# One 512 KB weight load moved from SyncE's DMA queue to ScalarE's, in a one-core hybrid attention layer

## The reference, cut to what matters

```
h   = rmsnorm(x, norm_pre_g)
u   = h @ w_in                       # 1024 x 4096: q, k, v and gate columns of two head groups
A   = differential attention, B = block-sparse attention, both with a relative position bias
y   = concat(A * silu(gate_a), B * silu(gate_b)) @ w_out
out = x + rmsnorm(y, norm_post_g)
```

## Time and profile before

| | |
|---|---|
| median of 3 runs | 254.0 us (253.83, 254.0, 255.63) |
| the profiled execution | 254.23 us |
| its span | 252.4 us |
| PE busy | 245.6 us, 97% of the span |
| DVE, ACT, POOL busy | 177.0, 143.0, 32.7 us |
| mean granted TensorE clock | 0.997 |
| DMA moved | 42.47 MB |

### The profile page before, as it was taken

How to read it: one execution, slowest core, us unless ns; L and a number is a source line. 1 busy time by engine, 2 the same in 40 slices (tenths; PEclk the granted TensorE clock), 3 DMA queues, 4 the chain that set the end, 5 groups by cost and what they waited for, 6 DMA issues and landing times.

```text
span 252.4 us, 4450 instructions
## 1 busy us (share of the span) xinstructions
PE 245.6 (97%) x1567; PEld 123.2 (49%) x1567; DVE 177.0 (70%) x393; ACT 143.0 (57%) x336; POOL 32.7 (13%) x74
## 2 busy tenths in 40 slices
PE   8999999999999999999999999999999999999991
PEld 6454444445444554544455444454444444555570
DVE  2998585587478688868877767977787896835313
ACT  4777565375356666574677595667565665611110
POOL 1329300000000320041031033000000000111101
PEclk9999999999999999999999999999999999999998
DMA  6978979605656545544935644568849869982422
GB/s 242 366 245 173 310 251 371 218 28 135 106 160 163 180 114 130 140 163 112 203 103 136 137 161 119 136 189 184 174 103 201 209 157 170 202 203 43 125 86 83
DMA packets 59674, 42.47 MB, mean 168 GB/s; under 512 B 45808, under 2 KB 46072, under 8 KB 59652
## 3 DMA queue, kind: packets, MB, share of 16 engines
q1 hardware_dynamic: 59636, 42.18, 63.5%
q10 hardware_dynamic: 16, 0.00, 0.0%
HBM read 29.04 MB, written 2.13 MB: 123 GB/s over the span
## 4 chain that ended last, share of the span: by engine, by line
PE 97%; DVE 1%; DVEq 0%; POOLq 0%; issue 0%; ACT 0%; POOL 0%; ACTq 0%
PE unit_ps L578 72%; PE score_ps L634 6%; PE o_ps L655 5%; PE unit_ps L608 4%; PE unit_ps L589 3%; PE unit_ps L615 2%; PE unit_ps L543 1%; PE score_ps L536 1%; PE score_ps L709 1%; PE unit_ps L709 1%; DVE area L1058 0%; DVE gates L956 0%; DVEq L180 0%; POOLq L180 0%; ACT junk L732 0%
## 5 line engine op out<-in xcount | busy, mean ns | idle before, releaser
L578 PE MATMUL unit_ps<-area,w_hi 128*128 128x512 f16 x256 | 76.2, 379 | 0.0
L788 ACT ACTIVATE arena<-arena,negmax 128x512 f32<-128x512 f32 (+3 forms) x64 | 35.4, 554 | 49.5 <-DVE negmax L985 49.4
L578 PE MATMUL unit_ps<-w_hi,area 128*128 128x512 f16 x192 | 60.3, 379 | 0.0
L578 PE MATMUL unit_ps<-area,w_lo 128*128 128x512 f16 x128 | 48.5, 379 | 0.0
L578 PEld LDWEIGHTS unit_ps<-area,w_hi 128*128 128x128 f16 x256 | 24.1, 98 | 27.2 <-issue 1.1
L578 PE MATMUL unit_ps<-w_lo,area 128*128 128x512 f16 x96 | 36.4, 379 | 0.0
L985 DVE CUSTOM_DVE_ANT_0 arena<-score_ps,strips 128x512 f32<-128x512 f32 (+3 forms) x64 | 28.6, 485 | 9.2 <-PE score_ps L634 9.2
L882 DVE SCALAR_TENSOR_TENSOR w_lo<-stage,g_cols,w_hi 128x512 f16<-128x512 f32 x32 | 24.2, 755 | 11.3 <-ACT w_hi L746 11.2
L578 PEld LDWEIGHTS unit_ps<-w_hi,area 128*128 128x128 f16 x192 | 18.8, 98 | 21.9 <-DVE w_lo L888 0.7
L745 ACT ACTIVATE w_hi<-stage,g_cols 128x512 f16<-128x512 f32 x32 | 22.7, 711 | 7.3 <-DMA stage<-in_w_in_dram 7.3
L884 DVE SCALAR_TENSOR_TENSOR w_lo<-stage,g_cols,w_hi 128x512 f16<-128x512 f32 x32 | 24.8, 777 | 0.0
(11 more groups left out here) (106 smaller groups left out, 357.7 us busy)
## 6 DMA issues: line engine op xcount, KB each, us to landing
stage<-in_w_in_dram SPq DMA_DIRECT2D x32, 512.0 KB, 4.3
stage<-in_w_out_dram SPq DMA_DIRECT2D x8, 512.0 KB, 4.2
arena<-in_x_dram SPq DMA_DIRECT2D x4, 512.0 KB, 5.2
strips<-bias_rows SPq DMA_DIRECT2D x4, 512.0 KB, 4.7
stage<-in_x_dram SPq DMA_DIRECT2D x4, 512.0 KB, 4.7
out_dram<-area SPq DMA_DIRECT2D x3, 512.0 KB, 2.7
strips<-bias_rows SPq DMA_DIRECT2D x1, 1024.0 KB, 7.8
pt<-arena SPq DMA_TRANSPOSE x32, 3.1
```

What stands on the lines that cost most here:

```text
L578: last = nc.tensor.matmul(bank, a, b, start=(k == 0 and n == 0), stop=(k == KT - 1 and n == 2))
L788: nc.scalar.activation(probs[:, i % 2, m, 0:n], probs[:, i % 2, m, 0:n], ACT.Exp, bias=negmax[:, i, m:m + 1], scale=-1.0, accum_out=sums[: ...
```

## The change

The load of quarter 0 leaves SyncE's queue. ScalarE issues the same transfer, to the same buffer and with the same semaphore, right behind the load of g and ahead of its first computation.

```diff
             load_x(0)
-            load_quarter(0)
             load_quarter(1)
             load_x(1)
             sp.wait_ge(x_loaded[0], 16)
...
             nc.scalar.dma_start(g_rows[:, :], norm_pre_g[0].rearrange("(k p) -> k p", p=P)).then_inc(gpre_loaded, 16)
+            first = GROUPS[0][2]
+            nc.scalar.dma_start(stage[:, 0, :].rearrange("p (k n) -> p k n", k=2),
+                                w_in_v[:, 0:2, first:first + WIDTH]).then_inc(w_loaded[0], 16)
             x_square(0)
             split(0)
             split(1)
```

## The result

The changed kernel takes 257.73 us (median of 6 runs, 257.52 to 259.2) against 254.07 us before (6 runs, 253.76 to 255.63): ratio 1.0144, 95% interval 1.0111 to 1.0178. It is 3.7 us slower, outside the predicted range of 253.4 to 256.0. The profiled execution took 259.2 us with a span of 257.4; it is the slowest of the six, 4.97 us over the profiled execution before, and the others lie near 257.6.

What follows compares the result with a forecast made beforehand. TensorE was taken to bound the kernel, so start delays reach the end. First product 0.35 us later, less 0.2 at quarter 2, gave +0.15 on the 254.0 median, rounded up to 254.2 us; range 253.4 to 256.0.

Steps and rivals of the forecast that it cites:

- What bounds the kernel: Whole kernel: TensorE, busy 230.90 of 230.90 us from 16.0 us, so a loss before 16 us arrives at the end one for one.
- What it costs to issue: Start, ScalarE and SyncE queues: quarter 0 issued 0.1 us later, quarter 1 and tile 1 0.46 us earlier; value 0.
- What it costs tile 0: First loads: quarter 0 shares the DMA engines with x's tile 0, which lands 0.5 us later (bounds 0 to +1.0).
- The lower bound of -0.1 us: Low end of the net +0.15 us at the start, for tile 0 undisturbed by quarter 0.
- Nothing moves: Rival, first loads: each DMA engine finishes tile 0, then takes quarter 0, as before; 254.23 or 254.0 us; chance 0.33.
- Quarter 0 becomes the late one: Rival, first loads: quarter 0 shares with tile 0, then quarter 1, landing after 6.35 us; +0.5 to +1.7 us; chance 0.12.
- the 0.2 at quarter 2: TensorE before 10.98 us: its wait for quarter 2, counted as 0.2 us and no longer waited when TensorE comes later.
- The clock rises late: Rival, TensorE's first products: idle behind late tile 0, clock rises late; price 1.7 to 2.6 us, time 256.1 to 257.4; chance 0.08.
- Hidden issue work on ScalarE: ScalarE's start: quarter 0's issue moves the table load's end to 3.0 to 3.2 us, hidden before 4.43.

## Why the prediction was wrong, step by step

*What bounds the kernel* held: the start alone matters, and a delay there reaches the end (231.30 of 231.30 us busy in the main part). What did not hold in general is its reverse: a gain at the start is capped at 29.23 us by the turning of tile 3.

*What it costs to issue* failed, and it is the step that decided. I took the issues as 0.1 us later for quarter 0 and 0.46 us earlier for quarter 1 and tile 1, each worth nothing. I had asked of the zero only what it does to quarter 2, never what it does to quarter 0. Together they were worth the whole loss: 1.18 for quarter 1 and 1.35 for quarter 0 put the one transfer with a hurry behind the one without, and tile 1, issued at 1.65, came close enough to share its engines. The sum put this at nothing. It is shown by the run in which 0.9 us of delay on SyncE's two transfers took the time back to 254.4, and the one in which tile 1 alone was held back (254.59) shows that quarter 1's place ahead of quarter 0 costs little by itself. No run delays quarter 1 and leaves tile 1 where it was, so what tile 1 costs alone is open.

*What it costs tile 0* was counted on the wrong transfer. Tile 0 stayed at 4.3 us. The sharing run by run, two thirds to the 4096-byte runs, was right, but it took place between quarter 0 and tile 1. Held back, tile 1 left quarter 0 at 6.8 us instead of 8.55: 1.75 us for the sharing, 1.1 for the place behind quarter 1 (6.8 against 5.7 before). The split holds for two queues; with all on one queue and tile 1 behind, the place cost 2.1 us. The lower bound of -0.1 us for an undisturbed tile 0 was a slip of its own: where nothing comes later, nothing is saved at quarter 2, and the sum is 0.

*Nothing moves* (0.33) took quarter 0 to follow tile 0 as before. Tile 0 was indeed left alone, but quarter 1 followed it.

*Quarter 0 becomes the late one* (0.12) was the right rival, mis-sized. "At worst it is done when quarter 1 is" took quarter 1's old arrival (8.23). Quarter 1 came at 6.0, in quarter 0's old place, and quarter 0 came last of the four (8.55, tile 1 at 8.35). The arrival's 2.33 us less the 0.2 at quarter 2 (0.28 by the rows) is +2.1, not at most +1.7. "It starts ahead of quarter 1 by half a transfer" was simply wrong: by my own figures quarter 1's issue stood ahead (1.19 against 1.30).

*The clock rises late* (0.08) was right in its mechanism and nearly in its price (1.7 to 2.6 us; the profiled execution lost 1.77 + 0.84 + 0.33 = 2.94), but I hung it on tile 0 and treated it as another case. It is the consequence of the case above: a gap of 3 us in front of TensorE. Its price in the median is 1.5 us, from the run with a busy TensorE; the run with the one-column activation gives as much between its own executions (256.0 against 257.5 and 257.7). The mean granted clock, 0.986 in the profiled execution and 0.99 to 0.992 in the five others, says that those lost less. Cases that cause each other must be added, not weighed: 2.1 + 1.5 = 3.6 us of the 3.7 measured.

*Hidden issue work on ScalarE* held: the table load ends at 3.08, tile 0 comes at 4.3.

## What to carry to other kernels

A second DMA queue is not a shortcut past the first. Before moving a transfer, write down all issues of all queues in order of time, and see that what is needed first is issued first, with a margin of more than a few tenths of a microsecond (here 0.15 us was not enough and 0.77 was); if a cheap wait can hold back a transfer that has time, that is worth more than a queue. And where TensorE waits some microseconds longer at the start, count the products behind the gap at half the clock as part of the same case, or give it work that nobody waits for.

## What the runs showed of the hardware

Transfers of three queues (SyncE, ScalarE, GpSimd) were begun in about the order of issue, even 4 KB behind 1.5 MB on other queues: g, issued at 1.25 us, landed at 6.8. Queues in progress together took turns run by run, 69 packets against 68. The Trainium skill, in "DMA: Bandwidth & Descriptors", section "Queues, rings and completion order", has an engine go round the queue rows for which it has work. If quarter 0's work had been there when quarter 1's was, it should by that have begun beside quarter 1 at 3.45 us and not at 4.44; the trace does not show when an engine has a transfer's work.

In the change all four first transfers were there 1.0 us sooner (8.55 us against 9.52 for tile 1 before), which no time here has used; with two queues it is not always so (tile 1 at 10.77 in the run with quarter 1 at 1.49). And an issue on ScalarE's queue did not wait for a table load in progress (issued at 1.43, load from 1.36 to 2.64).

Open: why two transfers issued 0.15 us apart left four engines up to 3.3 us behind the other twelve, and why the engines kept closer together in the change than before (quarter 1's semaphore rose from 5.54 to 5.99 us, from 6.25 to 8.21 before). No run here looks into the single engine.
